# Wave stages: the squares of the new stream kept in eight chunks and summed on TensorE, none added on GpSimd

## The reference

```python
def rms_norm(x, g):
    xf = x.astype(jnp.float32)
    y = xf * lax.rsqrt(jnp.mean(xf * xf, axis=-1, keepdims=True) + RMS_EPS)
    return (y * g.astype(jnp.float32)).astype(x.dtype)

x = x + gt1 * rms_norm(y, norm_g[i, 1])               # "post": norm of the mixer's output y, added to the stream
h = modulate(rms_norm(x, norm_g[i, 2]), sh2, sc2)     # "norm": norm of the new stream x
x = x + gt2 * rms_norm(squared_relu_mlp(h, mlp_w1[i], mlp_w2[i]), norm_g[i, 3])
```

## Time and profile before

| | |
|---|---|
| median of 3 runs | 4725.79 us (4725.38 to 4730.21) |
| profiled execution | 4725.82 us, span 4723.4 us |
| TensorE busy | 4512.8 us, 96% of the span |
| VectorE, ScalarE, GpSimd busy | 58%, 22%, 2% |
| granted TensorE clock, mean | 0.977 |

### The profile page before, as it was taken

The page is one execution under the profiler, slowest core; times in us unless marked ns, Lnnn a source line. Parts: engine busy times, 40 slices in busy tenths (PEclk is TensorE's granted clock), DMA queues, the critical chain, the costliest instruction groups (busy, mean ns, idle before and its releaser), DMA issues.

```text
span 4723.4 us, 70026 instructions
## 1 busy us (share of the span) xinstructions
PE 4512.8 (96%) x29686; PEld 3175.5 (67%) x29686; DVE 2723.4 (58%) x4919; ACT 1050.6 (22%) x2377; POOL 107.2 (2%) x105
## 2 busy tenths in 40 slices
PE   7999999999989999999999999989999999989998
PEld 4555655555547667757885888546886888545886
DVE  3173545536347777645555666674657666674666
ACT  1053000002036666631002010241001010251000
POOL 0001000001000000000000000110000000110000
PEclk9999999999999999998999999989999999989999
DMA  5210222211200000111222222202222222201221
GB/s 242 94 77 36 89 107 107 107 54 54 85 1 3 3 3 3 39 61 74 89 90 75 85 77 81 89 36 86 80 85 83 87 82 72 105 36 71 90 89 45
DMA packets 27045, 339.07 MB, mean 72 GB/s; under 512 B 3024, under 2 KB 3024, under 8 KB 6896
## 3 DMA queue, kind: packets, MB, share of 16 engines
q1 hardware_dynamic: 24048, 324.51, 18.2%
q0 software_dynamic: 2688, 10.09, 0.6%
HBM read 330.40 MB, written 4.19 MB: 71 GB/s over the span
## 4 chain that ended last, share of the span: by engine, by line
PE 86%; DVE 8%; ACT 3%; issue 2%; DMA 1%; POOL 0%; SPq 0%; ACTq 0%; DVEq 0%; POOLq 0%
PE ps L1497 46%; PE ps L1115 21%; PE ps L1124 2%; PE ps L1700 1%; PE ps L1631 1%; PE ps L1672 1%; PE ps L1683 1%; PE ps L1168 1%; ACT arena L2035 1%; PE ps L1430 1%; PE ps L1760 1%; DMA arena<-in_panels 1%; DVE arena L3279 1%; PE ps L1562 1%; PE ps L1717 1%
## 5 line engine op out<-in xcount | busy, mean ns | idle before, releaser
L1497 PE MATMUL ps<-arena 128*128 128x256 f32 (+1 forms) x9096 | 2116.4, 395 | 20.9 <-DVE arena L3004 20.9
L1497 PEld LDWEIGHTS ps<-arena 128*128 128x128 f32 x9096 | 1734.4, 191 | 390.5 <-DVE arena L3004 23.4
L1115 PE MATMUL ps<-arena 128*128 128x512 f32 (+3 forms) x2800 | 1041.3, 532 | 2.2 <-ACT arena L1986 1.8
L1115 PEld LDWEIGHTS ps<-arena 128*128 128x128 f32 x2800 | 525.7, 192 | 501.7 <-issue 442.0
L2995 DVE TENSOR_TENSOR arena<-ps,arena 128x512 f32<-128x512 f32 (+1 forms) x250 | 157.5, 630 | 319.2 <-PE ps L1497 317.4
L2995 DVE TENSOR_TENSOR square<-ps,square 128x512 f32<-128x512 f32 (+1 forms) x145 | 99.0, 683 | 176.5 <-PE ps L1497 176.4
L2936 DVE TENSOR_TENSOR arena<-arena 128x1024 f32<-128x1024 f32 (+2 forms) x153 | 190.4, 1244 | 5.0 <-ACT arena L1986 1.7
L2188 ACT COPY square<-ps 128x512 f32<-128x512 f32 (+1 forms) x65 | 37.2, 573 | 656.3 <-PE ps L1497 587.8
L2188 ACT COPY arena<-ps 128x384 f32<-128x384 f32 (+1 forms) x35 | 18.5, 529 | 575.2 <-PE ps L1497 549.4
L3287 DVE COPY_PREDICATED arena<-const,ps 128x256 f32<-128x256 int32 x192 | 83.7, 444 | 75.6 <-PE ps L1700 70.1
L2035 ACT ACTIVATE arena<-arena,state_sum 128x256 f32<-128x256 f32 (+2 forms) x128 | 76.5, 598 | 216.5 <-DVE state_sum L2617 214.4
(11 more groups left out here) (375 smaller groups left out, 4974.8 us busy)
## 6 DMA issues: line engine op xcount, KB each, us to landing
arena<-in_panels SPq DMA_DIRECT2D x144, 2048.0 KB, 7.8
arena<-in_panels SPq DMA_DIRECT2D x9, 1536.0 KB, 6.4
arena<-in_bias POOLq DMA_DIRECT2D x8, 512.0 KB, 6.0
arena<-in_x_in SPq DMA_DIRECT2D x1, 3072.0 KB, 10.7
x_save<-arena POOLq DMA_DIRECT2D x1, 2048.0 KB, 7.5
arena<-x_save POOLq DMA_DIRECT2D x1, 2048.0 KB, 13.9
out_x<-arena SPq DMA_DIRECT2D x8, 256.0 KB, 2.2
arena<-in_panels SPq DMA_DIRECT2D x1, 1792.0 KB, 11.7
```

The lines of the kernel that those rows point to most:

```text
L1115: ins = pe.matmul(dest, left(k), right(k), start=(k == 0), stop=(k == nk - 1))
L1497: ins = pe.matmul(bank[:, j * cut.side:(j + 1) * cut.side], left[:, k, j * P:(j + 1) * P], right[k], start=(k == 0), stop=(k == cut.rows - 1))
```

## The change

The square of each new chunk of X is written to its own place, chunk c of H, which the next step overwrites anyway with the scaled X. GpSimd adds nothing any more, and ScalarE doesn't wait for it. TensorE sums all eight chunks itself (`norm_sum`): 4 x 8 narrow matmuls for the latents, 2 x 8 for the context. It waits for each chunk's square separately. In `turn` the latents' 32 are split in two runs of 16, with column 2 of w1 between them. The "post" norms stay as they were (`post_sum` is the old `wave_sum` for them).

```diff
@@ gpsimd
-            def norm_gather(v):
-                a, b = WAVES[v]
...
-                for c in range(1, KD - 1):
-                    pool.wait_ge(sem("squared"), base + c + 1)
...
-                    pool.tensor_tensor(rstd[:, a:b], rstd[:, a:b], square[:, c % 2, a:b], ALU.add).then_inc(
-                        sem("norm_gathered"), one("norm_gathered"))
@@ tensor
+            def norm_sum(v, chunks):
+
+                a, b = WAVES[v]
+                if chunks[0] == 0:
+                    stat_bank_free()
+                for c in chunks:
+                    pe.wait_ge(sem("squared"), more("squared"))
+                    for t in range(a // P, b // P):
+                        ins = pe.matmul(ps[:, 4, 0:TILES], H[:, c, t * P:(t + 1) * P], to_column(t),
+                                        start=(t == a // P and c == 0), stop=(t == b // P - 1 and c == KD - 1))
+                if chunks[-1] == KD - 1:
+                    ins.then_inc(sem("summed"), one("summed"))
@@ turn
-                columns(w1, [0, 1, 2], src, context)
-                wave_sum("norm", 0)
+                columns(w1, [0, 1], src, context)
+                norm_sum(0, range(4))
+                columns(w1, [2], src, context)
+                norm_sum(0, range(4, KD))
                 columns(w1, [3], src, context)
                 wave_row(0)
@@ first_up (k == 4) and odd_in
-                        wave_sum("norm", 1)
+                        norm_sum(1, range(KD))
@@ scalar
                 act.wait_ge(sem("x_chunk"), n["x_chunk"] + KD * v + c + 1)
-                if c >= 3:
-                    act.wait_ge(sem("norm_gathered"), n["norm_gathered"] + (KD - 2) * v + c - 2)
-                act.activation(square_dest(c)[:, a:b], X[:, c, a:b], ACT.Square).then_inc(
+                act.activation(H[:, c, a:b], X[:, c, a:b], ACT.Square).then_inc(
                     sem("squared"), one("squared"))
```

More of the change, by code:

```diff
@@ L1044, in begin @@
                 mod(0, 0, 4)
-            def norm_gather(v):
-                a, b = WAVES[v]
-                base = n["norm_squares"]
-                n["norm_squares"] += KD
-                for c in range(1, KD - 1):
-                    pool.wait_ge(sem("squared"), base + c + 1)
-                    if c > 1:
-                        pool.wait_ge(sem("norm_gathered"), n["norm_gathered"])
-                    pool.tensor_tensor(rstd[:, a:b], rstd[:, a:b], square[:, c % 2, a:b], ALU.add).then_inc(
-                        sem("norm_gathered"), one("norm_gathered"))
[L1058 to L1064, removed]
             def odd_in():
@@ L1069, in odd_in @@
                 pool.dma_start(x_save, X[:, :, 0:LAT]).then_inc(sem("x_saved"), 16)
-                norm_gather(1)
             def odd_out():
@@ L1088, in _ @@
             model(dict(load=load, begin=begin, mod=mod, gains=skip, norm_mod=skip, even_in=even_in, attention=attention, project=skip,
-                       post=skip, out_turn=out_turn, mlp=mlp, odd_in=odd_in, prep=skip, scan=skip, feature=skip, readout=skip, fill=skip, odd_out=odd_out, enter=skip, swiglu=swiglu, final=skip,
+                       post=skip, out_turn=skip, mlp=skip, odd_in=odd_in, prep=skip, scan=skip, feature=skip, readout=skip, fill=skip, odd_out=odd_out, enter=skip, swiglu=swiglu, final=skip,
                        mix_in=conv_taps, conv=skip, store=skip))
@@ L1228, in gathered_sum, with post_sum @@
                 ins.then_inc(sem("summed"), one("summed"))
-            def wave_sum(kind, v):
+            def post_sum(v):
                 a, b = WAVES[v]
-                squares, gathered = dict(post=("square", "gathered"), norm=("squared", "norm_gathered"))[kind]
                 stat_bank_free()
-                pe.wait_ge(sem(squares), more(squares, KD))
-                pe.wait_ge(sem(gathered), more(gathered, KD - 2))
+                pe.wait_ge(sem("square"), more("square", KD))
+                pe.wait_ge(sem("gathered"), more("gathered", KD - 2))
                 for t in range(a // P, b // P):
@@ L1258, in turn @@
                 columns(w0, [0], src, context)
-                wave_sum("post", 0)
+                post_sum(0)
                 columns(w0, [1], src, context)
@@ L1281, in first_up @@
                     if k == 0:
-                        wave_sum("post", 1)
+                        post_sum(1)
                     elif k == 2:
@@ L1960, in turn @@
                 n["gathered"] += 2 * (KD - 2)
-                n["norm_gathered"] += 2 * (KD - 2)
             def out_turn():
```

## The result

The changed kernel takes 4742.77 us (median of 6, 4732.6 to 4744.1), the kernel before 4725.59 us (median of 6, 4720.17 to 4730.21). The ratio is 1.0032, 95% interval 1.0022 to 1.0042: slower by 0.3%, near the 4744 us of the forecast. The medians lie 17.2 us apart; the ratio amounts to 15.1 us (10.4 to 19.8). The profiled execution took 4742.53 us.

What follows compares the result with a forecast made beforehand. TensorE, busy 96% of the span, was taken as the bound. Sums less waits, +11.7 us, and the clock, +6.9, made +18.6 on 4725.82: 4744 us, 0.4% slower, with an 8-in-10 range of 4733 to 4756.

Steps and rivals of the forecast that it cites:

- What bounds it: Whole kernel: TensorE is busy 96% of the span, so a turn's gain or loss is carried to the end in full.
- Wave 0, +7.0: Latents' sums, both turns: 24 additional sums cost 5.35 us per turn, less waits of 1.84 and 1.83 us; +7.0 us.
- Wave 1, +4.7: Context sums: 12 additional sums cost 2.68 us per turn, less a 0.67 us wait in turn 1; +2.0 and +2.7 us.
- VectorE and GpSimd: Both waves: 24 GpSimd adds and stretching of VectorE's add go, worth nothing beyond waits of 1.84, 1.83 and 0.67 us.
- The clock, +6.9: Behind runs of sixteen sums: one slow stretch more in wave 0 and one in wave 1, each turn; 4 x 1.73 us.
- slow stretch: TensorE work slowed by a fallen clock, such as a column taking 5.22 us instead of 3.49; priced at 1.73 us.
- the last two stay, as their idle times do: Each turn's slow stretches at the next product's beginning and behind the idle time before the context product remain.
- Rival 1 and 2: Two turns: 1, no further clock loss, 4737.5, chance 0.17; 2, narrow matmuls count as work, two stretches vanish, 4734.0, chance 0.12.
- Rival 3: Seam of each run with a column: additional sums cost next to nothing, their loads hidden; 4721.6 us, chance 0.03.
- Rival 4: Both turns: clock falls at every run, stays down over column between and sums; at most 4757.5 us, chance 0.12.

Runs made afterwards that it cites:

- the kernel with two chunks: Changed kernel, but only the first and last of the new stream's eight chunks of squares summed, part of the computation left out: 4719.81 us, ratio 0.9982 to the kernel before.
- pairs: Kernel before, but in wave 0 VectorE adds the squares in four pairs and TensorE sums two runs of 8; wave 1 unchanged: 4719.80 us, ratio 0.9983.
- the kernel before with wide sums: Kernel before with only the new stream's 24 sums widened from 6 to 120 columns: 4723.23 us, ratio 0.9992.

## Why the prediction was right

- *What bounds it.* TensorE in both turns, every gain or loss carried to the end: the offset was 6.6 us from 482 to 1075 us, and 17.0 at the end after 18.0 at 1179.93.
- *Wave 0, +7.0.* Measured +6.7. The second sixteen started at 430.19 us where 430.5 was forecast, and no square was waited for. A sum is 0.218 us on average in a run of sixteen: the first takes less than the others, which are 0.223 apart.
- *Wave 1, +4.7.* Measured +4.5.
- *VectorE and GpSimd.* The stretching of the adds is gone in all of them, and taking GpSimd out was worth about the waits and the stretches behind them: 7.4 us in the kernel with two chunks, against 7.8. By the Trainium skill (SBUF — State Buffer, "SBUF: two separate sides") the shared port pair is what had stretched them; the trace agrees, 0.68 us without GpSimd and 1.17 beside it, while VectorE's L2707, which reads PSUM for one operand, keeps 0.68 us beside GpSimd too (417.67 us). The advice that could be read from it was right, and the price of following it in this way was higher.
- *The clock, +6.9.* Measured +7.1 in the turns of the profiled execution, where "narrow matmuls do not hold the clock" was the mechanism. The price of four slow stretches was right and their places were not: I had one more in wave 0 of each turn, and it was none in turn 1 and two stretches' worth in turn 2, with a run partly at half speed (4.31 us). Counted as falls there are five instead of today's two, so three more, and one of them lasted twice as long. For falling, the mechanism was tested by width alone and holds. That such sums don't raise the clock rests on the row at 2128 us and was not tested.
- *What the prediction had wrong.* A slow stretch costs 1.69 us and not 1.73: the normal column behind sums is 3.54 us from start to start (405.54 to 409.08). And "the last two stay, as their idle times do" failed once: in turn 2 the one at the context product went (14.05 us instead of 15.74), which gave 1.7 us back. The sum had 18.6, the span grew by 17.0. The row of wave 0 in turn 1 stands at 438.90 us, just ahead of the forecast 439 to 443, since no further fall came there.
- *Rival 1 and 2* fell with the long rows behind the runs (5.39, 8.81, 5.39, 6.37, 8.81); only in wave 0 of turn 1 was it as rival 1 had it. The Trainium skill (TensorE: Matmul & The Clock Gate, "What's actually happening") has activity release the throttle: if the profile's busy share is taken for activity, the trace disagrees, since TensorE was busy throughout; 120 columns for 6 at the same length and busy share kept the clock. *Rival 3* fell with 0.218 us a sum, seams included. *Rival 4*, the clock down over the column between and the sums, came nearest in turn 2, where the clock fell at both runs; but it was back at 1.00 from 1098 to 1100 us, when the second run began.

What I was lucky in: the sum of four slow stretches, which came about in other places than forecast. The changed kernel's six runs span 11.5 us, with a fastest one of 4732.6 that was not traced; fewer falls may be why. What stays open is why not every run of sixteen loses the clock (ten of the twelve in the three traces that have them did, not the first of turn 1 in the two that have it), what decides at the start of the next product, and where pairs gain 3 us more.

## What to carry to other kernels

A busy share of 100% does not say that a stretch keeps the clock: look at the columns of its matmuls too. Here a run of narrow matmuls cost its length plus, at sixteen in a row and not at eight, the slowing of the full work behind it. Breaking the runs up with full columns removed that; so did letting the same matmuls stream more columns, which cost no time here. Moving reductions to the engine that sets the end is dear even when it removes waits. Pairing wave 0's squares on an engine with idle time (VectorE), so that TensorE summed half as many tiles there, and leaving wave 1 on GpSimd beat both the kernel before and the change.

## What the runs showed of the hardware

Within a run, sums with 120 moving columns start 0.223 us apart (431.24 to 432.58 us, seven starts, in the kernel before with wide sums), and so do sums with 6 (429.01 to 430.35 us in the kernel before). The moving columns don't set the length. Weight loads are busy for all 3.40 us of a window inside a run at either width, which points to the load of the 128 stationary columns; a fixed cost of each matmul is not ruled out. At the 0.50 clock the six-column sum takes 0.431 us. The operand with a repeated axis (six columns read 20 times) ran as any other. Eight narrow sums lost the clock with a wait of 1.84 us before them, kept it without the wait, and kept it with the wait when they were wide.
